# A two-block transformer kernel on one core: scores, top-k rounds and angles earlier on VectorE, rotated keys by DMA

## The reference, cut to what matters

```python
z = rmsnorm(x) @ w_in                      # a_q, a_k, a_v, i_q, i_k, i_w, c_q, c_kv, k_r, g
# branch a: each query attends to its 64 best keys
score = einsum('bqh,bqhs->bqs', iw, relu(iq . ik))     # 4 index heads, causal
_, sel = lax.top_k(score, 64)
logits = q . k_sel * 64**-0.5 + bias(rel_bias, distance)
# branch b: latent attention, 8 heads of 64 + 32 (rotated) features
q_nope, q_rope = split(rmsnorm(c_q) @ w_uq);  q_rope = apply_rope(q_rope, cos, sin)
k_nope, v_b    = split(rmsnorm(c_kv) @ w_ukv); k_rope = apply_rope(k_r, cos, sin)   # one k_rope for all heads
logits = (q_nope . k_nope + q_rope . k_rope) * 96**-0.5, causal
# then gates, w_out, a feed-forward block; then the second block (two layers, not touched here)
```

## Time and profile before

| | |
|---|---|
| median of 3 executions | 986.94 us (985.64 to 987.56) |
| the profiled execution | 985.64 us |
| its span, first to last instruction | 983.8 us |
| mean granted TensorE clock | 0.987 of full speed |
| PE busy | 946.4 us, 96% of the span |
| DVE busy | 736.5 us, 75% |
| ACT busy | 551.3 us, 56% |
| HBM traffic | 161.03 MB read, 3.01 MB written |

### The profile page before, as it was taken

The page is one execution under the profiler, slowest core; times in us unless marked ns, Lnnn a source line. Parts: engine busy times, 40 slices in busy tenths (PEclk is TensorE's granted clock), DMA queues, the critical chain, the costliest instruction groups (busy, mean ns, idle before and its releaser), DMA issues.

```text
span 983.8 us, 17668 instructions
## 1 busy us (share of the span) xinstructions
PE 946.4 (96%) x6896; PEld 874.0 (89%) x6896; DVE 736.5 (75%) x1574; ACT 551.3 (56%) x1108; POOL 128.6 (13%) x131
## 2 busy tenths in 40 slices
PE   7978999999999999999999999999897999999997
PEld 7978889999999988879999999899786999999997
DVE  7889755677766665886888777778898478877773
ACT  6666654555545546785555444448798364544444
POOL 3010001310000003003122221110000112222221
PEclk8999999999999999999999999999999999999999
DMA  8994334496545553315955555547211265555521
GB/s 278 239 218 133 129 130 164 140 257 226 200 172 187 198 172 130 129 45 185 282 189 195 187 176 202 180 172 257 86 45 44 87 214 182 203 172 190 196 86 43
DMA packets 25988, 165.18 MB, mean 168 GB/s; under 512 B 3321, under 2 KB 3705, under 8 KB 7473
## 3 DMA queue, kind: packets, MB, share of 16 engines
q1 hardware_dynamic: 23504, 156.09, 46.8%
q0 software_dynamic: 2400, 7.97, 4.4%
HBM read 161.03 MB, written 3.01 MB: 167 GB/s over the span
## 4 chain that ended last, share of the span: by engine, by line
PE 80%; DVE 10%; ACT 7%; issue 1%; DMA 1%; POOL 0%; SPq 0%; DVEq 0%; ACTq 0%
PE bank L547 21%; PE bank L550 11%; PE bank L570 10%; PE bank L574 9%; PE bank L572 9%; PE bank L521 4%; PE bank L525 4%; PE bank L529 4%; DVE lo L1628 3%; ACT PN L1346 2%; PE bank L532 1%; PE bank L533 1%; ACT hi L1105 1%; PE bank L538 1%; DMA stage<-in_stream 1%
## 5 line engine op out<-in xcount | busy, mean ns | idle before, releaser
L1628 DVE TENSOR_TENSOR lo<-stage,hi 128x1024 fp32r<-128x1024 f32 x291 | 346.9, 1222 | 11.2 <-ACT hi L1105 11.1
L1105 ACT ACTIVATE hi<-stage 128x1024 fp32r<-128x1024 f32 x291 | 295.8, 1044 | 15.1 <-PE bank L574 12.7
L547 PE MATMUL bank<-HT,hi 128*128 128x512 f32 x920 | 230.6, 392 | 0.0
L547 PEld LDWEIGHTS bank<-HT,hi 128*128 128x128 f32 x920 | 165.5, 189 | 29.6
L570 PE MATMUL bank<-UH,hi 128*128 128x256 f32 x608 | 172.4, 283 | 2.9 <-ACT UH L1416 2.9
L574 PE MATMUL bank<-UL,hi 128*128 128x256 f32 x608 | 172.3, 283 | 0.0
L572 PE MATMUL bank<-UH,lo 128*128 128x256 f32 x608 | 172.0, 283 | 0.0
L550 PEld LDWEIGHTS bank<-HT,lo 128*128 128x128 f32 x920 | 125.5, 190 | 9.0
L550 PE MATMUL bank<-HT,lo 128*128 128x256 f32 x920 | 128.3, 282 | 0.0
L570 PEld LDWEIGHTS bank<-UH,hi 128*128 128x128 f32 x608 | 116.7, 192 | 3.2 <-issue 3.2
L574 PEld LDWEIGHTS bank<-UL,hi 128*128 128x128 f32 x608 | 116.7, 192 | 0.2
(11 more groups left out here) (319 smaller groups left out, 1575.2 us busy)
## 6 DMA issues: line engine op xcount, KB each, us to landing
stage<-in_stream SPq DMA_DIRECT2D x144, 1024.0 KB, 4.9
BT<-scratch POOLq DMA_DIRECT2D x8, 256.0 KB, 16.2
BT<-scratch POOLq DMA_DIRECT2D x4, 512.0 KB, 19.3
stage<-in_stream SPq DMA_DIRECT2D x3, 512.0 KB, 9.3
scratch<-VR POOLq DMA_DIRECT2D x2, 768.0 KB, 20.8
XT<-in_xt SPq DMA_DIRECT2D x4, 256.0 KB, 6.8
B<-scratch POOLq DMA_DIRECT2D x4, 256.0 KB, 7.5
out<-ROWS SPq DMA_DIRECT2D x4, 256.0 KB, 2.4
```

The lines of the kernel that those rows point to most:

```text
L547: e.matmul(out[:, 0:512], hi[:, j % HI_SLOTS, 128 * k:128 * k + 128], HT[:, :, k, :], start=k == 0, stop=False)
L1105: e.activation(hi[:, j % HI_SLOTS, 0:w], stage[:, j // 2 % ST_PAIRS, j % 2, 0:w], ACT.Copy).then_inc(*up("hi", ("hi", j, 0)))
L1628: e.tensor_tensor(lo[x], stage[x], f32(hi[:, j % HI_SLOTS, 0:sched[j][2]]), ALU.subtract).then_inc(*up("lo", ("lo", j, 0)))
```

## The change

Four things are done to the first block:

- The rotated keys are no longer copied by ACT. DVE writes their sum once, and SP waits for it and issues two DMAs of 256 KB from it into K96, ahead of the load of pair 10. PE, ACT's later gates and POOL wait for these DMAs ("k rope").
- The eight score instructions of DVE stand ahead of the key tile instead of behind query head 3. One of the splits that stood ahead of the key tile and one behind the first scaled latent now both stand behind the score.
- Two of the eight top-k rounds stand ahead of DVE's copies of the keys; six are left for `pairs`.
- The last seven angle steps stand in the start-up.

```diff
@@ first_products, tensor
-                    for key in (("q96", h, 0), ("q96", h, 1), ("k96", h), ("k rope", h // 4)):
+                    for key in (("q96", h, 0), ("q96", h, 1), ("k96", h), ("k rope",)):
@@ scalar
-        def rotated_keys(i):
-            q.wait_ge(*at("kr"))
-            e.activation(K96[64:128, 4 * i:4 * i + 4, :], KR[64:128, 0:1, :].to_broadcast([64, 4, 256]), ACT.Copy).then_inc(*up("key", ("k rope", i)))
         slabs.splits(1)
-        rotated_keys(0)
...
         all_of(latent_queries(0))
-        rotated_keys(1)
         slabs.splits(1)
@@ vector
         for k in range(4, 8):
             low_row(rows, k, gain(0, k))
+        some_angle(2)
         low_split(1)
         slabs.begin(2)
         slabs.splits(1)
+        some_angle(99)
         slabs.flush()
...
         slabs.splits(2)
-        some_angle(99)
         slabs.give(one_tile("cq", 1))
...
-        slabs.flush(1)
+        q.wait_ge(*at("iw"))
+        q.wait_ge(*at("index relu", 1))
+        q.wait_ge(*at("index relu", 2))
+        for h in range(4):
...
+            e.scalar_tensor_tensor(SC[:, 0:256], R1[:, h, :], iwt[:, 1, h:h + 1], causal[:, 0:256] if h == 0 else SC[:, 0:256], ALU.mult, ALU.add).then_inc(*up("step", ("score", 0, h)))
...
+            e.scalar_tensor_tensor(SC[:, 256:384], R0[:, h, :], iwt[:, 0, h:h + 1], causal[:, 256:384] if h == 0 else SC[:, 256:384], ALU.mult, ALU.add).then_inc(*up("step", ("score", 1, h)))
...
+        slabs.splits(1)
         j = one_tile("kr", 0)
...
-        e.tensor_tensor(KR[96:128, 0, :], KR[64:96, 0, :], KR[64:96, 1, :], ALU.add)
         e.tensor_tensor(KR[64:96, 0, :], KR[64:96, 0, :], KR[64:96, 1, :], ALU.add).then_inc(*up("step", ("kr",)))
...
-            if c == 2:
-                slabs.splits(1)
...
         all_of(tile_in_parts("g", 1, gate_out))
+        topk_round()
+        topk_round()
...
         all_of(latent_queries(0))
         slabs.splits(1)
-        q.wait_ge(*at("iw"))
-        q.wait_ge(*at("index relu", 1))
-        q.wait_ge(*at("index relu", 2))
-        for h in range(4):
...
@@ gpsimd
         q.wait_ge(*at("tables"))
+        q.wait_ge(*at("k rope"))
         choose()
@@ sync
         for j in range(1, len(sched), 2):
+            if j == slab["kr", 0] + 1:
+                q.wait_ge(*at("kr"))
+                for c in (64, 96):
+                    load(K96[c:c + 32, :, :], KR[64:96, 0:1, :].to_broadcast([32, 8, 256]), "keys", *[("k rope",)] * (c == 96))
             load_pair(j // 2 + ST_PAIRS)
```

More of the change, by code:

```diff
@@ L168 @@
     "w0", "w1", "w2", "w3", "w4", "w5", "wone2", "wfirst0", "wfirst1", "x0", "x1", "x2", "x3", "columns", "masks",
-    "positions", "columns2", "tables", "scratch", "bias", "bias2", "bias3", "compress", "out",
+    "positions", "columns2", "tables", "scratch", "keys", "bias", "bias2", "bias3", "compress", "out",
 )
@@ L212, in next_high, with flush @@
         self.todo.append(j)
-    def flush(self, n=None):
-        now, self.todo = (self.todo, []) if n is None else (self.todo[:n], self.todo[n:])
-        for j in now:
+    def flush(self):
+        for j in self.todo:
             self.low(j)
             self.lows.add(j)
+        self.todo = []
     def splits(self, n):
@@ L1290, in open_gate @@
             if i >= 8:
-                for part in range(2):
-                    q.wait_ge(*at("k rope", part))
+                q.wait_ge(*at("k rope"))
                 for part in range(2):
@@ L1895, in vector @@
             e.tensor_scalar(DG[:, c, :], idc[:, 0:128], fc[:, c:c + 1], None, ALU.mult).then_inc(*up("root_dve", *[("latent diagonals",)] * (c == 3)))
-        slabs.flush(1)
+        q.wait_ge(*at("iw"))
+        q.wait_ge(*at("index relu", 1))
+        q.wait_ge(*at("index relu", 2))
+        for h in range(4):
+            if h:
+                q.wait_ge(*at("score", 0, h - 1))
+            e.scalar_tensor_tensor(SC[:, 0:256], R1[:, h, :], iwt[:, 1, h:h + 1], causal[:, 0:256] if h == 0 else SC[:, 0:256], ALU.mult, ALU.add).then_inc(*up("step", ("score", 0, h)))
+            if h:
+                q.wait_ge(*at("score", 1, h - 1))
+            e.scalar_tensor_tensor(SC[:, 256:384], R0[:, h, :], iwt[:, 0, h:h + 1], causal[:, 256:384] if h == 0 else SC[:, 256:384], ALU.mult, ALU.add).then_inc(*up("step", ("score", 1, h)))
         blocks = (slice(0, 256), slice(256, 384))
```

## The result

The changed kernel took 995.87 us in the median of four executions (993.81 to 997.14); the kernel before, beside it, 987.25 (985.64 to 988.14). The ratio is 1.0087, with a 95% interval of 1.0065 to 1.0109. That is 8.6 us slower, where the prediction said 991.0 us, 4.1 us slower, and at most 995.5. The direction was right, and so was what decides, the keys behind pair 9; the size was twice the forecast and left the range.

What follows compares the result with a forecast made beforehand. The prediction took DVE to set the pace from 45 to 100 us and PE after that. It summed 4.96 + 0.2 - 1.09 = +4.1 us on 985.64, giving 989.7, plus 1.30 to the median: 991.0 us, range 985.7 to 995.5.

Steps and rivals of the forecast that it cites:

- Landing 66.0 us: Rotated keys by DMA, queued behind pair 9: both loads have landed at 66.0 us, bounds 59.3 and 69.0.
- The four products take 2.1 us: PE's first attention products after the landing: about twice their 1.23 us at the lower clock, so top starts at 68.2.
- Top to head 6: 2.65 us: From DVE's first top to head 6 on PE: 2.65 us as before, so head 6 at 70.85.
- passes on whole: Behind head 6: DVE works without a break, so the delay of 4.96 us reaches the end undiminished.
- -1.09 us come back: Two top-k rounds gone from the third pair: PE's wait before the second branch's first product goes, gain 1.09 us.
- each microsecond of landing shifts the result by one: Sum of the forecast: a key landing one microsecond later or earlier moves the total time by one microsecond.
- +0.2; bounds 0 and +1.0: Angles moved to the start-up: cost 0.2 us, between 0 and 1.0, as DVE's waits hide most of it.
- the stop behind head 5 would shrink to 1.7, the clock would hold: New DVE order, if nothing else were late: PE's 4.3 us stop behind head 5 falls to 1.7, without clock loss.
- PE's wait grows to 3.2: Score and split ahead of the key tile: PE's wait of 1.0 us at CTL grows by 2.2 to 3.2.
- Rival 1: Keys landed by 61.4 us, half-clock stretch gone: not slower, -0.9 us, 986.0 us; chance 0.17.
- Rival 4: B1's loads starve SP's queue, so the keys land near 72: +10, 997 us; chance 0.07.
- the stop at 80 kept: PE's stop of 2.7 us at 80, before the moved rounds, stays and comes 4 to 5 us later.

Runs made afterwards that it cites:

- e1: The changed kernel with the rotated keys copied by ACT again and DVE's second sum back: 990.10 us, 1.0034 against the kernel before.
- e3: The changed kernel with the last seven angle steps back in their old place: 994.25 us, 1.0076 against the kernel before.
- e4: The changed kernel with keys by ACT and angles in their old place, so only the new DVE order is left: 988.36 us, 1.0017.
- e6: The changed kernel with one key load of 512 KB from 64 partitions instead of two of 256 KB; DVE writes the sum twice: 992.69 us, 1.0075.
- e7: The changed kernel with the two key loads issued by ACT on its own hardware queue instead of by SP: 1005.40 us, 1.0166.
- e12: The kernel before with only score and split moved ahead of the key tile; top-k rounds, angles and ACT's key copies as before: 988.82 us, 1.0029.
- e2: The kernel before with only the two key loads by SP added, DVE order as before: 995.77 us, 1.0094.
- e8: The changed kernel with the two larger scratch writes and B1's loads held until the keys landed, table rows in own buffers: 989.95 us, 1.0031.
- e10: The kernel before with three splits moved behind the first top, ahead of the query halves of heads 4 and 5; table rows in own buffers: 986.09 us.
- e13: The kernel before with the two key loads by SP, and the large scratch writes and B1's loads held until the keys landed: 985.96 us, 0.9995.
- e5: The changed kernel with the key loads issued ahead of pair 9 instead of ahead of pair 10: 991.77 us, 1.0057.

## Why the prediction was wrong, step by step

The forecast added 4.96 (head 6), 0.2 (start-up) and -1.09 to +4.07 us. The two profiled executions differ by 9.09. The 5.0 us between are found along PE's timeline.

1. **"Landing 66.0 us" was 3.1 us early (69.1, just past its own upper bound of 69.0).** This is the largest failed term. The mechanism stood as written: pair 9 held back by the scratch writes, the keys behind it. I had frozen the times of before. Pair 9 was issued 1.3 us later (44.62, before 43.29), as the table rows that release the scratch writes and the slab use that releases pair 9 both hang on the start-up, which the moved angles lengthen. It then took 20.7 us instead of 19.3 (+1.4), which stays unexplained: it took 19.0 to 19.6 in e1, e3, e4, e6, e7 and e12, and 21.5 in e2. And the keys took 3.8 us behind it, not 3.4 (+0.4). The distance held in the other traces: 3.6 (e2), 3.8 (e3), 3.0 (e6). The rule "the keys come 3 to 4 us behind pair 9" was good, and its anchor was not.
2. **"The four products take 2.1 us", top at 68.2.** From landing to top were 3.2 us, not 2.2: 0.14 until PE started, 2.55 for the products at clock 0.50, and the way to DVE. +1.0. The first latent products also lose clock now, but the wait for the keys covers that.
3. **"Top to head 6: 2.65 us"** held exactly (72.30 to 74.95). PE then needed 1.01 us, not 0.80, until DVE could start its query half: +0.2. DVE's half of head 6 is 9.27 us late (75.96 to 66.69), and the stop at 91.93 is late by 9.26: it "passes on whole", as predicted, as far as this stop.
4. **"-1.09 us come back"** failed: the wait went, but the time did not come back. The first product of the second branch, before and after:

```profile
100.61 0.92 PE L820 MATMUL bank<-AK,AQ 64*128 64x256 f32 x8 [1.09 <-DVE AQ L1717]
...
110.11 0.92 PE L820 MATMUL bank<-AK,AQ 64*128 64x256 f32 x8
```

   That is +9.50, so 1.3 us went there. Behind the stop at 91.93 the clock was 0.66 for 5 us; behind that of before it was 1.00. The other traces say what to make of it. From this stop to the second branch PE took 17.9 us in before, of which 1.1 were the wait; 16.6 in e4 and e8, with the rounds moved and no half-clock stretch; and 18.0 to 18.2 in ten traces with one (19.2 in e3, with a longer one). Five of these, e2 and e10 to e13, have all eight rounds in their old place, and none of the five has the wait. So the wait that I counted as a gain stands in one trace alone, that of the one execution with the rounds in their old place that kept its clock there. Where the clock holds, the moved rounds gain 1.3 us (17.9 against 16.6); where it falls, they gain nothing. The length of the stop doesn't decide it: the stretch came behind stops of 2.4 us, and not behind 3.3 in e8.
5. Behind 110 us the difference falls by 0.4 to the end. Half-clock stretches lie elsewhere in each execution there; I did not trace the 0.4.

Together 3.1 + 1.0 + 0.2 + 1.3 - 0.4 = 5.2, less the 0.2 for the start-up, which is now inside the first term: 5.0.

**How much of this is the landing?** The list compares two executions. e3 is the test, as its keys landed at 66.0. In its trace the late stop is 3.1 us earlier than in the changed kernel (88.80), but the second branch only 2.1 (107.99) and the end of the span 0.6 (992.3); over all executions e3 gains 1.1 to 1.6 us. So "each microsecond of landing shifts the result by one" holds to the stop and isn't shown behind it, where the clock gave part of it back. With the forecast's landing 3.4 us of the miss are left. In e3's trace the second branch starts 3.5 us behind the forecast's 104.5: 1.0 from the products, 0.2 from head 6 and 2.3 behind that, where item 4 lies; none of it comes from the DMAs.

**Angles: "+0.2; bounds 0 and +1.0".** Mis-sized. The five angle steps from 15.96 on took 0.96, 0.71, 0.78, 0.92 and 0.72 us beside GpSimd's additions; in the old place they took 0.44 (1.32 for three), 0.35, 0.29, 0.42 and 0.29. I had counted 1.4 us of them as hidden in DVE's waits, and at double time they filled all of these and more: the low part started at 20.11 (I said 18.5), and PE, at 20.57 before, at 21.79. The angles cost 1.1 us by the ratios of the changed kernel and e3, and 1.7 by those of e1 and e4; the intervals overlap in both pairs, and the first is within the noise. The traces are clearer. From the end of PE's long start-up wait, at 10.92 to 13.20 us, to the issue of pair 9 they show 30.2 to 31.4 us in the eight kernels with the old place and 32.2 to 32.4 in five with the new one, 1.5 us more in the mean. The bound of 1.0 named the cause and was itself too low. The Trainium skill ("SBUF — State Buffer", section "SBUF: two separate sides") says that DVE and GpSimd hold a shared pair of ports by turns, for a whole instruction, where DVE's has two inputs in SBUF or a two-port mode. The trace agrees: all five took 2.0 to 2.7 times as long, and in e5, where the last of them came behind the additions, it took 0.37 us. Three of them have one input tensor, and no run shows their mode.

**Order: "the stop behind head 5 would shrink to 1.7, the clock would hold", net -1.09.** By its own terms the 1.7 should read 1.9 (head 3 later by 3.2 us, "top" by 0.85). The net was wrong by some 2.3 to 2.8 us, as e4 lost 1.2 (median) to 1.7 (ratio). Two steps failed. "PE's wait grows to 3.2" was right in size (3.1), but I gave it no clock cost, though I had read in the earlier trace rows what a 4.3 us stop does; in e4 52.8 to 56.2 ran at 0.52. And I followed DVE alone: ACT stood 0.97 us ahead of DVE's first minimum before, its chain (query copy, key copy, split, table load) starts when PE ends head 3, and that is what came late. In e4's trace head 6 is 1.36 us late and the second branch 0.02 us late. Counted from its own start-up, 1.1 us ahead, these are 2.4 and 1.1 us. Its span is 1.1 us longer, and that arises behind 370 us, in half-clock stretches whose place changes between executions. The loss over all executions is measured; how it divides in the others stays open.

**Rival 1 (keys in time: -0.9 us)** could be run, as e8 and e1: +3.4 and +2.9 us in the medians. Even with the keys in time the change would have been slower, so this rival's price was wrong by some 4 us: it stands on the same -1.09 and the same 0.2 as the forecast. The fit beside this rival (the Trainium skill, "DMA: Bandwidth & Descriptors", section "Anatomy of one DMA") is given there for DMAs that GpSimd issues, while SP issues these. With the engines free, 256 KB took 3.9 us in e8. **Rival 4** (B1's loads starve SP's queue) did not come: B1's loads started at 63.67, behind the scratch writes; they took 12.8 us each in the median instead of 6.4 to 8.1, so it was they that shared. **Right:** the key sum (done at 52.8 forecast, 53.9 measured, late with the start-up), the keys as the decider, the stop at 80 kept, slower.

**The cost by parts**, from the ratios, one on top of the other: the order 0.17% (e4), 1.7 us; the angles 0.17% more (e1), 1.7 us; the key loads 0.53% more (changed kernel), 5.2 us. Together 8.6. They are known to about 1, 1.6 and 2.5 us only, and the intervals of e4 and e1 overlap. Alone the loads cost as much as all together (e2, 8.6 us in the medians): without the other two PE comes to the products sooner, and waits 11.0 us there instead of 6.5.

## What to carry to other kernels

A transfer's price is that of its queue and of the engines at that moment: read how long the neighbours took just there, find what they wait for, and move that anchor by all that the same change delays ahead of it. A stop of PE often costs twice: behind the stops of 2.4 to 17 us here the clock stood at its lower level in most traces, so a stop that a forecast adds needs a second term for that. A short wait read in one profile is a gain only if it stands in other executions too. And when work is moved between two engines that feed a third, follow both, since the one that had the small slack (ACT's 0.97 us) comes to set the end.

## What the runs showed of the hardware

- From 44 to 51 us the software queue moved 0.72 MB at 96.8% of the engines, about 100 GB/s, while SP's pair 9, issued at 44.62, was pending and moved nothing. The source of those writes is one row per partition in 8 or 16 partitions. A 1 MB slab took 4.8 us with them out of the way (e8) and 20.7 beside them.
- A second hardware queue was no way past: 23.1 us for 256 KB on ACT's queue (e7), against 14.4 behind pair 9 on SP's. Beside each other the two hardware queues moved 392 and 324 packets, of 1 and about 7 KB.
- The issue of the second key load held SP for 3.55 us in the changed kernel, 4.41 in e2 and 4.52 in e5, and 0.60 in e8, with the engines free. In e5 only the first key load stood ahead in the queue, and e6's single load of 512 KB took 0.69 us behind pair 9, so what sets it stays open.
- 128 x 256 float32 steps on DVE took 0.71 to 0.96 us beside GpSimd's additions of the same shape, and 0.29 to 0.44 elsewhere.
